# Delta rule of a two-block model: the triangular inverse worked in halves of two chunks, another order of the state's products, and no state behind the last chunk

## The reference, cut to what matters

```python
L = where(strict, einsum('bhnid,bhnjd->bhnij', kb, k) * decay, 0.0)
M = L + eye(CHUNK)
sol = triangular_solve(M, concat([vb, kb * exp(gc)]), lower=True, unit_diagonal=True)
u, w = sol[..., :dv], sol[..., dv:]
qk = einsum('bhnid,bhnjd->bhnij', q, k) * decay
def step(state, inp):
    v_new = u_c - einsum('bhck,bhkv->bhcv', w_c, state)
    o_c = einsum(qd_c, state) + einsum(qk_c, v_new)
    state = state * gl_c + einsum('bhck,bhcv->bhkv', kd_c, v_new)
    return state, o_c
```

## Time and profile before

| | us |
|---|---|
| median of 3 runs (3107.21 to 3108.49) | 3107.44 |
| the profiled execution | 3106.88 |
| its span, first to last instruction | 3105.0 |
| TensorE busy | 3023.3 (97%) |
| DVE busy | 1904.8 (61%) |
| ScalarE busy | 1150.4 (37%) |
| GpSimd busy | 523.9 (17%) |

### The profile page before, as it was taken

How to read it: one execution, slowest core, us unless ns; L and a number is a source line. 1 busy time by engine, 2 the same in 40 slices (tenths; PEclk the granted TensorE clock), 3 DMA queues, 4 the chain that set the end, 5 groups by cost and what they waited for, 6 DMA issues and landing times.

```text
span 3105.0 us, 47808 instructions
## 1 busy us (share of the span) xinstructions
PE 3023.3 (97%) x18448; PEld 2610.7 (84%) x18448; DVE 1904.8 (61%) x2665; ACT 1150.4 (37%) x1987; POOL 523.9 (17%) x530
## 2 busy tenths in 40 slices
PE   8998999999999999999999999999999999999998
PEld 8997679999999888989886777888887787788886
DVE  7955676857564566857576565444579766654444
ACT  4234443322244665422233333222333544332223
POOL 4400213300011433410000001000034232200001
PEclk9999999999999999999999999999999999999999
DMA  3221012222232111222232222222222100022222
GB/s 134 88 90 41 18 38 75 88 89 88 93 99 83 48 44 59 95 90 93 92 99 93 90 81 82 95 95 95 95 95 88 61 1 1 28 95 95 95 94 83
DMA packets 71078, 241.04 MB, mean 78 GB/s; under 512 B 8336, under 2 KB 13456, under 8 KB 70928
## 3 DMA queue, kind: packets, MB, share of 16 engines
q1 hardware_dynamic: 69648, 234.75, 23.0%
q0 software_dynamic: 1280, 4.20, 0.5%
HBM read 231.51 MB, written 2.10 MB: 75 GB/s over the span
## 4 chain that ended last, share of the span: by engine, by line
PE 82%; DVE 10%; issue 4%; ACT 3%; DVEq 1%; POOL 0%; DMA 0%; SPq 0%; ACTq 0%; POOLq 0%
PE ps L274 45%; PE ps L303 21%; DVE conv_acc L350 3%; PE ps L799 3%; PE ps L2079 1%; PE ps L2086 1%; PE ps L1311 1%; PE ps L1720 1%; PE ps L1265 1%; DVE w_low L233 1%; DVE conv_in L337 1%; PE ps L1297 1%; PE ps L1291 1%; DVE conv_acc L347 1%; ACT w_high L228 1%
## 5 line engine op out<-in xcount | busy, mean ns | idle before, releaser
L274 PE MATMUL ps<-x_hi,w_high 128*128 128x264 f32 (+2 forms) x2712 | 705.3, 318 | 14.8 <-DVE x_lo L369 12.0
L274 PE MATMUL ps<-x_lo,w_high 128*128 128x264 f32 (+2 forms) x2712 | 702.1, 317 | 0.0
L274 PE MATMUL ps<-x_hi,w_low 128*128 128x264 f32 (+2 forms) x2712 | 700.5, 316 | 0.0
L228 ACT ACTIVATE w_high<-w_raw 128x1024 fp32r<-128x1024 f32 x426 | 446.8, 1050 | 414.7 <-DMA w_raw<-in_slabs 414.1
L233 DVE TENSOR_TENSOR w_low<-w_raw,w_high 128x1024 fp32r<-128x1024 f32 x346 | 439.2, 1269 | 205.0 <-ACT w_high L228 204.9
L274 PEld LDWEIGHTS ps<-x_hi,w_high 128*128 128x128 f32 x2712 | 448.4, 189 | 58.0 <-issue 11.0
L274 PEld LDWEIGHTS ps<-x_lo,w_high 128*128 128x128 f32 x2712 | 447.8, 189 | 34.0 <-issue 1.0
L274 PEld LDWEIGHTS ps<-x_hi,w_low 128*128 128x128 f32 x2712 | 448.5, 190 | 33.2
L350 DVE SCALAR_TENSOR_TENSOR conv_acc<-conv_in,par,conv_acc 128x528 f32<-128x528 f32 (+1 forms) x320 | 371.0, 1159 | 47.4 <-DVE conv_acc L347 4.4
L446 POOL TENSOR_TENSOR sqa<-sqa,rvar 128x512 f32<-128x512 f32 (+2 forms) x31 | 42.0, 1355 | 1361.6 <-ACT rvar L438 1360.3
L380 DVE TENSOR_TENSOR h<-ps,h 128x512 f32<-128x512 f32 (+1 forms) x120 | 83.2, 693 | 288.8 <-PE ps L274 201.6
(11 more groups left out here) (418 smaller groups left out, 4672.3 us busy)
## 6 DMA issues: line engine op xcount, KB each, us to landing
w_raw<-in_slabs SPq DMA_DIRECT2D x426, 512.0 KB, 3.5
rel_bias<-in_rel POOLq DMA_DIRECT2D x16, 256.0 KB, 2.9
h<-in_x SPq DMA_DIRECT2D x4, 528.0 KB, 6.9
out_y<-h SPq DMA_DIRECT2D x8, 256.0 KB, 2.1
sb_q_swap<-mix_x SPq DMA_DIRECT2D x16, 100.0 KB, 2.2
rel_k_swap<-mix_x SPq DMA_DIRECT2D x16, 96.0 KB, 2.5
mix_b<-mix_x SPq DMA_DIRECT2D x16, 64.0 KB, 2.1
rel_q_swap<-mix_x SPq DMA_DIRECT2D x16, 64.0 KB, 2.0
```

The source lines that it names most:

```text
L228: act.activation(w_high[:, n % RING, :], w_raw[:, n % RING, :], ACT.Copy).then_inc(S("w_hi"), 1)
L274: mm = pe.matmul(ps[:, 2 * tslot + k, 0:n], w, a[:, kb, c:c + n], start=first, stop=fin)
```

## The change

Inverse: the two halves of a head, chunks 0, 1 (q = 0) and chunks 2, 3 (q = 1), get signals of their own, and each half a bank of its own: the products of L2079 and the transposes of L2091 go to bank b0 + 2q, those of L2086 to b0 + 1 + 2q. ScalarE's copy, DVE's subtraction, DVE's copy and the making of the first XM become two instructions of 256 columns each. GpSimd still waits for both halves and handles four chunks at once. At level 1, TensorE waits in addition until PM has been made (`dn_pm`), as it now writes to bank b0 + 3. State: the product of the state with QG moves ahead of L2104's, and starts the sum; the state's product (L2111) moves ahead of vnew with PM (L2108), for both heads. Behind the last chunk the state's product and the new state are left out, and `dn_sp` is then signalled by the output's product.

```diff
+        def half(t, q):
+            return t[:, 2 * q:2 * q + 2, :].rearrange("p a b -> p (a b)")
+        def bank_half(bank, q):
+            return ps[:, bank + 2 * q, 2 * P * q:2 * P * q + 2 * P]
...
                 for k in range(1, 7):
                     for z, hh, b0, w in both:
                         pe.wait_ge(S("dn_lk"), 12 * pr + 2 * (k - 1) + z + 1)
-                        pe.wait_ge(S("dn_xm"), 12 * pr + 2 * (k - 1) + z + 1)
-                        for c in range(CH):
-                            mm = pe.matmul(ps[:, b0, P * c:P * c + P], w[KB][:, c, :], w[XM][:, c, :], start=True, stop=True)
-                        mm.then_inc(S("dn_pw"), 1)
+                        for q in range(2):
+                            pe.wait_ge(S("dn_xm"), 24 * pr + 4 * (k - 1) + 2 * z + q + 1)
+                            for c in (2 * q, 2 * q + 1):
+                                mm = pe.matmul(ps[:, b0 + 2 * q, P * c:P * c + P], w[KB][:, c, :], w[XM][:, c, :],
+                                               start=True, stop=True)
+                            mm.then_inc(S("dn_pw"), 1)
...
                 for c in range(CH):
                     if c:
                         for z, hh, b0, w in both:
-                            pe.wait_ge(S("dn_state"), 8 * pr + 2 * (c - 1) + z + 1)
+                            pe.wait_ge(S("dn_state"), 6 * pr + 2 * (c - 1) + z + 1)
                             pe.matmul(ps[:, b0, 0:P], kc(hh, c), state[z][:], start=True, stop=True).then_inc(S("dn_ks"), 1)
+                        for z, hh, b0, w in both:
+                            pe.matmul(ps[:, b0 + 2, P * c:P * c + P], state[z][:], w[QG][:, c, :], start=True, stop=False)
...
+                    for z, hh, b0, w in both if c < CH - 1 else ():
+                        pe.wait_ge(S("dn_vnew"), 8 * pr + 2 * c + z + 1)
+                        pe.matmul(ps[:, b0 + 3, 0:P], w[KD][:, c, :], vnew[z][:], start=True, stop=True).then_inc(S("dn_sp"), 1)
                     for z, hh, b0, w in both:
                         pe.wait_ge(S("dn_vnew"), 8 * pr + 2 * c + z + 1)
-                        pe.matmul(ps[:, b0 + 2, P * c:P * c + P], vnew[z][:], w[PM][:, c, :], start=True, stop=c == 0)
-                        if c:
-                            pe.matmul(ps[:, b0 + 2, P * c:P * c + P], state[z][:], w[QG][:, c, :], start=False, stop=True)
-                        pe.matmul(ps[:, b0 + 3, 0:P], w[KD][:, c, :], vnew[z][:], start=True, stop=True).then_inc(S("dn_sp"), 1)
+                        mm = pe.matmul(ps[:, b0 + 2, P * c:P * c + P], vnew[z][:], w[PM][:, c, :], start=c == 0, stop=True)
+                        if c == CH - 1:
+                            mm.then_inc(S("dn_sp"), 1)
...
@@ ScalarE @@
-                        act.wait_ge(S("dn_pw"), 14 * pr + 2 * k + z + 1)
-                        act.activation(w[DM][:].rearrange("p a b -> p (a b)"), ps[:, b0, :], ACT.Copy).then_inc(S("dn_w"), 1)
+                        for q in range(2):
+                            act.wait_ge(S("dn_pw"), 28 * pr + 4 * k + 2 * z + q + 1)
+                            act.activation(half(w[DM], q), bank_half(b0, q), ACT.Copy).then_inc(S("dn_w"), 1)
...
@@ VectorE @@
-                        dve.wait_ge(S("dn_px"), 12 * pr + 2 * (k - 1) + z + 1)
-                        v = w[XTM][:].rearrange("p a b -> p (a b)")
-                        dve.tensor_tensor(v, v, ps[:, b0 + 1, :], ALU.subtract).then_inc(S("dn_xt"), 1)
+                        for q in range(2):
+                            dve.wait_ge(S("dn_px"), 24 * pr + 4 * (k - 1) + 2 * z + q + 1)
+                            v = half(w[XTM], q)
+                            dve.tensor_tensor(v, v, bank_half(b0 + 1, q), ALU.subtract).then_inc(S("dn_xt"), 1)
...
-                    for z, hh, b0, w in both:
+                    for z, hh, b0, w in both if c < CH - 1 else ():
                         dve.wait_ge(S("dn_sp"), 8 * pr + 2 * c + z + 1)
```

More of the change, by code:

```diff
@@ L2076, in dn_pe @@
                         pe.wait_ge(S("dn_lk"), 12 * pr + 2 * (k - 1) + z + 1)
-                        pe.wait_ge(S("dn_xm"), 12 * pr + 2 * (k - 1) + z + 1)
-                        for c in range(CH):
-                            mm = pe.matmul(ps[:, b0, P * c:P * c + P], w[KB][:, c, :], w[XM][:, c, :], start=True, stop=True)
-                        mm.then_inc(S("dn_pw"), 1)
-                    for z, hh, b0, w in both:
-                        pe.wait_ge(S("dn_w"), 12 * pr + 2 * (k - 1) + z + 1)
-                        if pr and k == 1:
-                            pe.wait_ge(S("dn_oln"), 2 * pr - 2 + z + 1)
-                        for c in range(CH):
-                            mm = pe.matmul(ps[:, b0 + 1, P * c:P * c + P], w[DM][:, c, :], w[XTM][:, c, :], start=True, stop=True)
-                        mm.then_inc(S("dn_px"), 1)
@@ new lines, in dn_pe @@
+                    for z, hh, b0, w in both:
+                        if k == 1:
+                            if pr:
+                                pe.wait_ge(S("dn_oln"), 2 * pr - 2 + z + 1)
+                            pe.wait_ge(S("dn_pm"), hh + 1)
+                        for q in range(2):
+                            pe.wait_ge(S("dn_w"), 24 * pr + 4 * (k - 1) + 2 * z + q + 1)
+                            for c in (2 * q, 2 * q + 1):
+                                mm = pe.matmul(ps[:, b0 + 1 + 2 * q, P * c:P * c + P], w[DM][:, c, :], w[XTM][:, c, :],
+                                               start=True, stop=True)
+                            mm.then_inc(S("dn_px"), 1)
```

40 lines of the change are left out of this document (23 added, 17 removed).

## The result

The changed kernel takes 3088.98 us, median of 7 runs (3088.22 to 3099.41), against 3107.21 (3106.38 to 3108.49, 7 runs) before: the medians lie 18.2 us apart. The ratio on record, which counts every run, is 0.9947, 95% interval 0.9938 to 0.9956. One of the seven, the 3099.41, had a mean granted clock of 0.944, the other six 0.995 (3088.22 to 3090.64). The forecast was 3093.1, so the gain is 4 us larger than forecast.

A forecast was written before the change was run, and what follows sets the result against it. TensorE was taken as the bound, busy 97%, with time won only where it waits, 0.94 per level. Inverse 9.4 plus state 4.9 gave 14.3 us off 3107.4, forecast 3093.1, range 3086.5 to 3099.5.

The forecast's parts named there:

- A level in halves: Inverse, plain level: halves let DVE subtract at 2.51 and the next level start about 4.70 instead of 5.34, gain 0.64.
- What gets in the way: Inverse: GpSimd's cut blocks DVE's second instruction; gain only 0.21 behind level 1, 0.11 behind levels 3 and 4, pairs 2 to 4.
- X: Inverse: time of DVE's first subtraction in a level, from its first weight load; 2.51 plain, 3.29 behind levels 3 and 4.
- X + 4 x 0.35 + 0.42 + 0.12: Inverse: end of a level whose first DVE subtraction is late, with eight halves at spacing: 1.94 behind that subtraction.
- The state: State steps: period 2.77 instead of 3.20, 1.0 per pair; with the earlier last copy at the ends, 4.9 us together.
- the step on the end: End of the state: ScalarE's second square 0.67 after the first, last copy leaves DVE at 3.06 instead of 3.33, gain 0.27.
- The clock: TensorE's granted clock, which fell at two of three changes of pair before; the forecast counted no gain from it.
- rival 2: Changes of pair: better filled TensorE loses both clock falls, about 3.3 more off, 3090; a third fall costs 1.7; chance 14%.
- rival 1: Inverse: DVE's second instruction is granted before GpSimd, all five intervals give 0.64, 19.3 us off, 3088; chance 14%.
- Rival 3: Inverse: halves dear on DVE (0.52, spacing 0.45), plain intervals give 0.42, inverse about 2.5, with the state 3101; chance 12%.
- 4: Inverse: each TensorE group beginning with a wait costs 0.12, 12 groups a level instead of 6, slower, 3114; chance 5%.
- Without the rule: Inverse: levels' gain put at 13.7 us if GpSimd and two-input DVE instructions did not block each other on the shared port.

The follow-up runs named there:

- e4: Changed kernel with GpSimd's cuts for levels 2 to 6 reduced to one column of one chunk: 3089.32 us, ratio 0.9936.
- e3: Kernel before the change with only the state's product and new state behind the last chunk left out: 3105.39 us, ratio 0.9993.
- e1: Changed inverse in halves alone, with the state as in the kernel before the change: 3098.25 us, ratio 0.9966.
- fill: Changed kernel with two more unused products for each head on TensorE at each change of pair: 3089.93 us, ratio 0.9946.
- e2_state: Kernel before the change with the changed state alone, inverse in whole heads as before: 3099.93 us, ratio 0.9974.

## Why the prediction was right, and where its sizes were off

- **A level in halves: right, 0.60 of 0.64.** DVE's first subtraction was at 2.54 (forecast 2.51), its length 0.41 on average (0.42), its spacing 0.33 (0.35), the next level at 4.75 (4.70).
- **What gets in the way: mechanism right, two sizes off.** That behind level 1 the cut would get in ahead of the second query was right. The step "L2312 holds from 0.87 to 1.60, GpSimd waits and then runs to 1.60 + 1.15 = 2.75" was not: DVE was free at 0.79, not 0.87, and the cut ended at 2.67 (1.24 + 1.43). L2335 ended 3.22 behind the start, and DVE's next instruction could start 0.08 before that, at 3.14, where the step had X = 3.29. The rule "X + 4 x 0.35 + 0.42 + 0.12" gives 1.94 behind X and measured 1.85: four spacings of 0.33 take 0.08 less, and the rest is rounding. What the step had right is that the cut ends 1.15 behind L2312's end (1.14 measured) and L2317 0.55 behind the cut's. So 4.99 instead of 5.23 six times, and 4.94 instead of 5.13 four times: 2.2 us more than forecast. The plain intervals (ten, 0.045 each) and level 6 (four, 0.05) take 0.65 back: 9.4 becomes 10.9. e4 shows that the rest of the long intervals is the cut's price and nothing else.
- **The state: 5.7 for 4.9.** The list gave 2.77, the trace 2.73, 0.1 a pair. The change of pair gave 0.39 for 0.27; what the step on the end missed was "the second 0.67 later": with the two outputs side by side it is 0.50. e3 shows what share the last state has: 0.25 of the change of pair and no part of the steps.
- **The clock: taken as unchanged, gave 1.5.** The forecast put this term at nothing, and rival 2 had its size about right (1.7 a fall forecast, about 1.5 measured). Its reason, that a better filled state would keep the clock, is neither shown nor excluded. For it: with the state's old order 6 of 9 changes of pair had a fall (before, e1, e3), with the new one and no fill 10 of 27, and on one and the same chip the mean granted clock was 0.9940 over the 20 runs of before and 0.9954 over the nine of e2_state. Against it: that split of falls comes by chance in 12 of 100 cases, and e3_last, without the new order, had one fall and, on that chip too, a mean clock of 0.9947 over its ten runs.
- **The rivals.** 1 (GpSimd not in the way, 3088) is out although its time is the one measured: the long intervals are there, and e4 shows what they would be without. 3 fell by the 0.415. 4 fell by the fence of the plain level: groups of two behind a wait each, and 0.89 for eight loads, against 0.88 before. A wait that had been fulfilled cost TensorE no more than that 0.01 here.
- **Sums that do not come out.** "Without the rule the levels' gain would be 13.7" should be 20 x 0.64 + 4 x 0.37 = 14.3, which is what rival 1's 19.3 rests on. Rival 3's inverse of "about 2.5" would give 3100; by its own terms (ten intervals that give 0.42, ten that lose 0.3 to 0.4, level 6) it is about 1.7, which fits its 3101. And 3099.5, the upper end of the range, is not halfway towards rival 3 (that would be 3097) but four fifths of the way. None of them moves the forecast.

In the profiled execution 18.7 us went where 14.3 were forecast. Of the 4.4 between them, 1.5 are the inverse, 0.7 the state, 1.5 the clock, 0.3 the work ahead of the stretch and some 0.4 the end and what lies outside the span. So half of the distance is sizes of the forecast's terms, and the other half is terms that it put at nothing: the clock, whose cause is open, and spread, which is luck. The 3089 lies next to the times of rivals 1 and 2 (3088 and 3090) as well; only the intervals, with e4, tell the forecast's mechanism from rival 1's.
